# A transformer block on one core: Strassen's scheme in the down projection for 18 pairs of weight tiles where it was 16

## What is computed

```python
x = x + mix @ w_out[l]                       # retention and sliding-window heads before it
h = rms_norm(x, ln2[l])
u = h @ w_ffn_in[l]                          # 2048 x 11264
a, b = jnp.split(u, 2, axis=-1)
a = causal_depthwise_conv(a, conv_w[l], conv_b[l])
x = x + (jax.nn.gelu(a, approximate=False) * b) @ w_ffn_out[l]      # 5632 x 2048: the down projection
return rms_norm(x, ln_f)
```

## Time and profile before

| | |
|---|---|
| time, median of 3 runs | 1112.03 us (1111.85 to 1113.12) |
| the profiled execution | 1111.31 us |
| its span | 1109.5 us |
| matmuls on TensorE | 5698 |
| down projection | from 869.4 us on; sweep 1 from about 985 us |
| instructions | 16360 |

### The profile page before, as it was taken

The page is one execution under the profiler, slowest core; times in us unless marked ns, Lnnn a source line. Parts: engine busy times, 40 slices in busy tenths (PEclk is TensorE's granted clock), DMA queues, the critical chain, the costliest instruction groups (busy, mean ns, idle before and its releaser), DMA issues.

```text
span 1109.5 us, 16360 instructions
## 1 busy us (share of the span) xinstructions
PE 1095.0 (99%) x5698; PEld 925.8 (83%) x5698; DVE 776.5 (70%) x1064; ACT 586.7 (53%) x792; POOL 75.3 (7%) x86
## 2 busy tenths in 40 slices
PE   8999999999999999999999999999999999999996
PEld 6888888888788888888888888888888888888885
DVE  5655666666655575656657656666577999989997
ACT  5445555555545545544545445455455665665662
POOL 2000111111100001101101011010010100000001
PEclk9999999999999999999999999999999999999998
DMA  9865555554566666666666666666666555755741
GB/s 340 259 189 171 154 163 158 151 162 159 153 184 180 188 176 188 189 190 188 188 189 189 189 189 188 186 186 187 186 186 192 178 188 197 240 184 184 262 156 76
DMA packets 146247, 206.90 MB, mean 186 GB/s; under 512 B 7539, under 2 KB 75537, under 8 KB 145952
## 3 DMA queue, kind: packets, MB, share of 16 engines
q1 hardware_dynamic: 145632, 204.67, 60.4%
q0 software_dynamic: 544, 1.72, 0.4%
q10 hardware_dynamic: 32, 0.01, 0.0%
HBM read 204.17 MB, written 2.10 MB: 186 GB/s over the span
## 4 chain that ended last, share of the span: by engine, by line
PE 97%; DMA 1%; DVE 1%; SPq 0%; ACT 0%; issue 0%; DVEq 0%
PE acc L690 15%; PE acc L470 13%; PE acc L472 13%; PE acc L471 13%; PE acc L696 8%; PE bank_s L690 7%; PE bank_tr L690 7%; PE bank_tr L696 4%; PE bank_s L696 4%; PE bank_s L470 2%; PE bank_s L472 2%; PE bank_s L471 2%; PE bank_tr L471 2%; PE bank_tr L472 2%; PE bank_tr L470 2%; DMA x_res<-in_x 1%
## 5 line engine op out<-in xcount | busy, mean ns | idle before, releaser
L1064 DVE TENSOR_TENSOR w_lo<-raw,w_hi 128x1024 fp32r<-128x1024 f32 x296 | 362.8, 1226 | 293.9 <-ACT w_hi L803 291.8
L803 ACT ACTIVATE w_hi<-raw 128x1024 fp32r<-128x1024 f32 x296 | 313.9, 1061 | 423.2 <-PE acc L472 168.1
L690 PE MATMUL acc<-h_both,w_hi 128*128 128x512 f32 x704 | 220.3, 394 | 0.0
L696 PE MATMUL acc<-h_both,w_lo 128*128 128x256 f32 x704 | 140.6, 282 | 0.0
L470 PE MATMUL acc<-w_hi,h_both 128*128 128x512 f32 (+1 forms) x352 | 139.2, 395 | 0.2 <-DVE h_both L1071 0.2
L472 PE MATMUL acc<-w_hi,h_both 128*128 128x512 f32 (+1 forms) x352 | 134.4, 382 | 0.0
L471 PE MATMUL acc<-w_lo,h_both 128*128 128x512 f32 (+1 forms) x352 | 134.2, 381 | 0.0
L690 PEld LDWEIGHTS acc<-h_both,w_hi 128*128 128x128 f32 x704 | 121.1, 190 | 15.1
L696 PEld LDWEIGHTS acc<-h_both,w_lo 128*128 128x128 f32 x704 | 121.0, 190 | 13.7
L690 PE MATMUL bank_s<-h_both,w_hi 128*128 128x512 f32 x352 | 109.1, 391 | 0.0
L690 PE MATMUL bank_tr<-h_both,w_hi 128*128 128x512 f32 x352 | 109.0, 391 | 0.0
(11 more groups left out here) (250 smaller groups left out, 1654.0 us busy)
## 6 DMA issues: line engine op xcount, KB each, us to landing
raw<-in_w_ffn_in SPq DMA_DIRECT2D x176, 512.0 KB, 3.6
raw<-in_w_ffn_out SPq DMA_DIRECT2D x88, 512.0 KB, 4.5
raw<-in_w_in SPq DMA_DIRECT2D x128, 256.0 KB, 3.0
raw<-in_w_out SPq DMA_DIRECT2D x32, 512.0 KB, 3.9
raw<-in_w_in SPq DMA_DIRECT2D x20, 512.0 KB, 8.7
x_res<-in_x SPq DMA_DIRECT2D x4, 512.0 KB, 9.7
decay<-table_decay POOLq DMA_DIRECT2D x1, 1024.0 KB, 9.3
lnf_row<-in_ln_f SPq DMA_DIRECT2D x1, 1024.0 KB, 8.2
```

Source lines behind the costliest of these rows:

```text
L690: mm(out, w_hi[:, slot, q * COLS + ft * P:q * COLS + (ft + 1) * P], h_both[:, 2 * k + q, :, :].rearrange("p a n -> p (a n)"), start=k == 0 ...
L696: ins = mm(out, w_lo[:, slot, q * COLS + ft * P:q * COLS + (ft + 1) * P], h_hi[:, 2 * k + q, :], start=False, stop=k == 7 and q == 1, skip ...
L803: run(w_hi[:, n % SPLIT, :], raw[:, n % RAW, :], ACT.Copy).then_inc(hi_ready, 1)
L1064: tt(w_lo[:, n % SPLIT, :], raw[:, n % RAW, :], w_hi[:, n % SPLIT, :].bitcast(F32), ALU.subtract).then_inc(lo_ready, 1)
```

## The change

Two constants change. `S_PAIRS` goes on to pair 19 of each sweep (9 pairs in a sweep in place of 8), and `others_out` of sweep 0 stands behind pair 21's `lo_pair` and no longer behind pair 20's, because the shared products are now complete two pairs later. That of sweep 1 stays behind pair 43's. `g_sums` grows from 8 to 9 slots. SyncE's loads come in the order of before; it also waits for the weight sums of pair 19 before it fills that pair's places in `raw` again.

```diff
-S_PAIRS = list(range(3, 18, 2))
+S_PAIRS = list(range(3, 20, 2))
 S_SLOT = {pair: i for i, pair in enumerate(S_PAIRS)}
 S_SUMS = 4
 X_ADDS = 6
-X_OUT_AT = (20, 43)
+X_OUT_AT = (21, 43)
 GAIN_AT = 18
```

## The result

The changed kernel takes 1114.79 us (median of 21 runs, 1113.31 to 1117.74) against 1111.85 us (21 runs, 1111.33 to 1114.24) in the same series: ratio 1.0028, 95% interval 1.0022 to 1.0034. It is slower by 2.9 us, where the prediction had 1.85; the lowest runs of the two differ by 1.98 us. The same kernel, measured in a second series, gave 1113.62 against 1111.78 us, ratio 1.0019 (1.0010 to 1.0029). The profiled execution took 1114.61 us, its span 1112.7.

The account below looks back on a forecast made before the run. VectorE's queue was taken to bound the end: 4.79 us more work, less 2.37 of waits, 0.49 from sweep 0 and 0.08 to spare, gave +1.85 us, so a median of 1113.9 us, range 1111.8 to 1115.0.

Parts of the forecast that it names:

- What bounds the end: At the last banks, VectorE's queue with `others_out` decides when the first addition starts; a fixed 15.9 us tail follows.
- The 4.79 us of a converted pair: Extra VectorE work per converted pair: weight sums 2.65, sums of g 0.47 and `t_lo` 1.67 us.
- `token_sums` costs nothing: Four operations of 1.22 us grow 0.15 us each, hidden by a 0.43 us wait; 0.6 us at most otherwise.
- Sweep 0 0.49 us sooner: TensorE saves 0.68 us in sweep 0 and loses 0.19 to pair 18's late, thin start, ending 0.49 us sooner.
- The move of `others_out` costs nothing: In sweep 0 it ends at 979.9 us, TensorE wants it about 984.7: 4.8 us of cover, no cost.
- The tie at pair 27's `t_lo`: VectorE still waits here for TensorE's pair 25, 0.3 us instead of 0.98, and so goes on 0.49 us sooner.
- Rival 3: Delay above 0.5 us at pair 27's `t_lo` removes VectorE's wait and reaches the end: 1114.4 to 1114.9 us; chance 0.13.
- The waits at pair 43 vanish, `others_out` 1.93 us later: In sweep 1 VectorE's extra work uses up 2.37 us of waits; `others_out` starts at 1090.0 instead of 1088.07.
- TensorE stands at tile 86: Six matmuls into pair 42, TensorE waits about 1.1 us for pair 43's `w_lo`, losing its 1.17 us lead.
- The sum: First addition of the last banks at 1095.44 instead of 1093.59 us: the kernel +1.85 us slower.
- the second condition of `others_out`: In sweep 1, pair 41 done on TensorE at about 1087.6 us, taken as met before the 1090.0 start.
- the 0.20 us a period: Per ordinary pair plus pair of seven, VectorE needs 10.40 us against TensorE's 10.20, so loses 0.20 us of lead.

Follow-up runs that it names:

- second_sweep: The kernel before with only sweep 1's pair 41 converted to a pair of seven, `others_out` of sweep 0 left behind pair 20: +2.33 us in the trace, ratio 1.0034.
- out21_before: The kernel before with only `others_out` of sweep 0 moved behind pair 21: -0.03 us in the trace, ratio 1.0004.
- out20_after: The changed kernel with `others_out` of sweep 0 put back behind pair 20: +7.38 us against the kernel before in the trace, ratio 1.0086.
- sums_after: The changed kernel with the next pair's weight sums behind `lo_pair` in VectorE's queue, no longer ahead: +0.60 us against the kernel before in the trace, ratio 1.0011.

## Why the prediction held

- **What bounds the end.** Right: VectorE's queue. The chain is its own from pair 27 to the last banks, and 2.41 us taken from that queue gave 1.50 back.
- **The 4.79 us of a converted pair.** Right: 9.7 us more busy time for two pairs. `second_sweep` alone: 4.79 - 2.37 - 0.08 = 2.34 expected, 2.33 measured.
- **`token_sums` costs nothing.** Right: its four operations take 1.35 us where they took 1.22, and the two executions are 1.32 us apart at the first of them (838.42 and 839.74) and 1.33 at the start of the down projection.
- **Sweep 0 0.49 us sooner.** Right. The ScalarE start that waits for its end, before and now, is 985.37 - 869.44 = 115.93 and 986.21 - 870.77 = 115.44 us behind the first matmul. Pair 18 started 0.08 us late and thin, as worked out.

```profile
985.37 0.63 ACT L970 ACTIVATE g_hi<-g_tok 128x512 fp32r<-128x512 f32 x1 [3.00 <-PE bank_s L472]
986.21 0.64 ACT L970 ACTIVATE g_hi<-g_tok 128x512 fp32r<-128x512 f32 x1 [3.00 <-PE bank_s L472]
```

- **The move of `others_out` costs nothing.** Right, `out21_before`. Its cover: taken away in `out20_after`, 7.38 us are lost, some 1.6 of them to the lower clock.
- **The tie at pair 27's `t_lo`.** Right, and near the edge: 0.24 us of wait left of 0.98, where the sum had 0.3. Rival 3 would have begun there, and in `sums_after` it did.
- **The waits at pair 43 vanish, `others_out` 1.93 us later.** 1091.32 - 870.77 = 220.55 against 1088.07 - 869.44 = 218.63: +1.92.
- **TensorE stands at tile 86.** 1091.46 - 1090.29 - 0.23 = 0.94 us where I had about 1.1.
- **The sum.** +1.85 predicted, +1.84 in the traces, and +1.84 us (1113.62 - 1111.78) in the second series of medians; that the medians agree to 0.01 us is luck, since the interval of that ratio is 1.1 to 3.2 us. The first series has 2.9. The difference, 1.1 us, is not of the down projection in any trace that was taken; the start of an execution scatters by up to 4 us, and unchanged code moved a ratio by 0.0011. That the excess of those 21 runs is of this kind is a likely reading, but their traces were not kept, so it stays open; also whether the program's layout has a part in it.
- **Missed:** the second condition of `others_out` (pair 41 done on TensorE) was in the text as met, and it was, by 1.4 us (ScalarE's copy starts at 1089.35 us and takes 0.60, `others_out` starts at 1091.32); I had not seen that it alone puts the kernel behind. And the 0.20 us a period that I took for a matter of throughput is, in sweep 0, a matter of order: with the sums behind `w_lo` TensorE loses nothing of it. With both pairs converted, the amount of work is the bound all the same: in `sums_after` VectorE has no wait left.

The rule of the Trainium skill (Perfetto Trace Analysis, Identifying the Most-Contended Engine), to make less work for the engine of the highest occupancy, led to the wrong sign here when it was taken over the whole span: TensorE got 1.36 us less, the kernel 1.84 us more. (For TensorE the same section of the Trainium skill does not go by the busy share of the matmuls but by that of the weight loads and by the share of peak; the weight loads' share is 83% here, still above VectorE's 70%.) Over 1009.65 to 1082.90 us both engines are full, and the trace agrees with a further point of the Trainium skill (Perfetto Trace Analysis, Optimization Strategy) that the engine which decides can change between stretches.

## What to carry to other kernels

A trade of work from a full engine to another is settled by the stretch where it is made, and at a kernel's end by what stands behind it in the other engine's queue: the same exchange was worth -0.54 us in the middle and +2.33 us two pairs from the end. Before taking work out of a queue that is only just too slow, look at its order: 2.65 us of sums moved behind the operation that the next engine waits for gave 1.50 us at no cost. To resolve less than 0.2%, compare traces from a common event behind the start-up; here that had a spread of 0.03 us, while two series of medians gave 2.9 and 1.8 us for the same change.

## What was not expected of the hardware

After a wait of 3.66 us of TensorE in the middle of dense work its clock was at the lower level for about 3 us, beginning 1.3 us after it had resumed; after a wait of 0.79 us it stayed at the full one. At the start of the program a fall followed waits of 1.43 and 1.74 us, 1.1 us apart, in one execution (`out21_before`), and none followed a wait of 1.41 us in another (before). Of the 4.0 us between these two, 1.5 are work at the lower clock and 2.5 stand ahead of it.
